# Mixture of experts, one core: the token rows of two expert blocks gathered by one 128-partition indirect DMA instead of two of 64

## The reference, cut to what matters

```python
g_p, g_idx = lax.top_k(g_probs, 1)                 # one of 4 groups
e_p, e_idx = lax.top_k(e_probs, TOP_K)             # two of its 8 experts
expert_idx = g_idx * EXPERTS_PER_GROUP + e_idx     # 32 experts in all
...
# for each expert: its tokens' rows, silu(x @ w_gate) * (x @ w_up) @ w_down,
# weighted and added back to the rows of its tokens
```

## Time and profile before

| | |
|---|---|
| Time, 3 runs | median 2164.02 us (2162.97 to 2166.41) |
| Profiled execution | span 2162.8 us from first to last instruction; its own time isn't listed apart from the span, which lies 0.2 us below the shortest of the 3 runs and 1.2 us below their median |
| PE busy | 2072.4 us, 96% of the span |
| DVE, ACT, POOL busy | 1186.1, 786.0, 176.5 us |
| Granted TensorE clock, mean | 0.986 |
| DMA | 357.61 MB, mean 165 GB/s |
| Expert stage | about 440 to 945 us |

### The profile page before, as it was taken

The page is one execution under the profiler, slowest core; times in us unless marked ns, Lnnn a source line. Parts: engine busy times, 40 slices in busy tenths (PEclk is TensorE's granted clock), DMA queues, the critical chain, the costliest instruction groups (busy, mean ns, idle before and its releaser), DMA issues.

```text
span 2162.8 us, 24857 instructions
## 1 busy us (share of the span) xinstructions
PE 2072.4 (96%) x10090; PEld 1444.9 (67%) x10090; DVE 1186.1 (55%) x1798; ACT 786.0 (36%) x1199; POOL 176.5 (8%) x132
## 2 busy tenths in 40 slices
PE   6999999999999889889999999999999999999997
PEld 4787788843333333348657788888776677888885
DVE  6556534423333233366885864656677858646565
ACT  4546533312211111144673421222345734212233
POOL 1000000010000000000100110102001001101020
PEclk9999999999999999999999999999999999999999
DMA  5342243499999999942202222232222022222221
GB/s 193 117 150 75 78 175 116 157 359 408 406 408 400 398 410 415 421 153 79 72 1 78 90 95 97 87 101 98 96 100 71 2 78 96 95 97 87 101 95 52
DMA packets 41137, 357.61 MB, mean 165 GB/s; under 512 B 6320, under 2 KB 7512, under 8 KB 13376
## 3 DMA queue, kind: packets, MB, share of 16 engines
q1 hardware_dynamic: 36448, 342.99, 41.6%
q0 software_dynamic: 4288, 10.95, 1.7%
q10 hardware_dynamic: 288, 2.10, 0.2%
HBM read 354.94 MB, written 6.83 MB: 167 GB/s over the span
## 4 chain that ended last, share of the span: by engine, by line
PE 81%; DMA 9%; DVE 4%; ACT 3%; issue 2%; SPq 0%; DVEq 0%; ACTq 0%
PE bank L1103 40%; PE bank L2093 10%; PE bank L458 8%; DMA H<-in_expert_up_w 5%; PE bank L473 3%; PE bank L480 2%; DMA AUX<-in_expert_up_w 2%; DMA ring<-in_expert_up_w 2%; PE bank L1885 2%; PE bank L1870 1%; PE bank L1901 1%; PE bank L2118 1%; PE bank L1130 1%; PE bank L2186 1%; ACT S L1950 1%
## 5 line engine op out<-in xcount | busy, mean ns | idle before, releaser
L1103 PE MATMUL bank<-split_x_high,split_weights 128*128 128x512 f32 x1888 | 586.4, 390 | 0.1
L1103 PEld LDWEIGHTS bank<-split_x_high,split_weights 128*128 128x128 f32 x1888 | 354.4, 188 | 76.8 <-issue 3.3
L1364 ACT ACTIVATE split_weights<-ring 128x2048 fp32r<-128x2048 f32 (+1 forms) x113 | 211.1, 1868 | 532.5 <-PE bank L1103 467.7
L1356 DVE TENSOR_TENSOR split_weights<-ring,split_weights 128x2048 fp32r<-128x2048 f32 (+2 forms) x115 | 258.5, 2248 | 164.5 <-ACT split_weights L1364 164.4
L1103 PE MATMUL bank<-split_products,split_weights 128*128 128x512 f32 x1136 | 302.7, 389 | 0.0
L1103 PE MATMUL bank<-split_x_low,split_weights 128*128 128x512 f32 x736 | 286.3, 389 | 0.0
L1103 PEld LDWEIGHTS bank<-split_products,split_weights 128*128 128x128 f32 x1136 | 213.2, 188 | 44.6 <-issue 0.5
L2093 PE MATMUL bank<-split_x_high,split_weights 128*128 128x512 f32 x480 | 153.4, 398 | 6.7 <-DVE split_x_low L2295 6.7
L1103 PEld LDWEIGHTS bank<-split_x_low,split_weights 128*128 128x128 f32 x736 | 138.2, 188 | 28.4
L1080 POOL TENSOR_TENSOR QKVG<-QKVG 128x512 f32<-128x512 f32 x44 | 97.9, 2224 | 551.9 <-DVE QKVG L1567 466.6
L686 DVE SCALAR_TENSOR_TENSOR S<-S,stats,bank 64x512 f32<-64x512 f32 x32 | 23.6, 739 | 197.0 <-ACT S L810 197.0
(11 more groups left out here) (469 smaller groups left out, 3206.6 us busy)
## 6 DMA issues: line engine op xcount, KB each, us to landing
ring<-in_ffn_w_up SPq DMA_DIRECT2D x44, 1024.0 KB, 4.8
ring<-in_w_in SPq DMA_DIRECT2D x24, 1024.0 KB, 4.8
QKVG<-in_expert_gate_w SPq DMA_DIRECT2D x11, 2048.0 KB, 26.4
AUX<-in_expert_up_w SPq DMA_DIRECT2D x11, 2048.0 KB, 31.0
QKVG<-in_expert_down_w SPq DMA_DIRECT2D x11, 2048.0 KB, 33.1
MKV<-in_expert_gate_w SPq DMA_DIRECT2D x11, 2048.0 KB, 30.3
ring<-in_expert_up_w SPq DMA_DIRECT2D x11, 2048.0 KB, 35.8
ring<-in_expert_down_w SPq DMA_DIRECT2D x11, 2048.0 KB, 27.9
```

Of the source, the lines that this page charges most:

```text
L1103: mm = pe.matmul(acc[:, :], w[:, u, k, m], x, start=first and q == 0, stop=last and q == 2)
L1356: st.tell(dve.tensor_tensor(w[:, 1, 0:ks, 0:nc_], raw_half(g)[:, :, 0:nc_], as_f32(w[:, 0, 0:ks, 0:nc_]), ALU.subtract), wl_done)
L1364: st.tell(act.activation(WHL[g % 2][:, 0, 0:ks, 0:nc_], raw_half(g)[:, :, 0:nc_], ACT.Copy), wh_done)
```

## The change

From the fifth block on, one indirect DMA gathers the rows of two blocks: blocks 2i and 2i+1 are pair i, the even one in partitions 0 to 63 and the odd one in 64 to 127. There are two buffers for pairs (`XB_PAIR`): pairs of even number land in `gatew`, those of odd number in `S[:, 8:10, :]`, where all the blocks were before. Blocks 0 to 3 and the further blocks are gathered as before. The index columns of pairs are laid out so that one column of 128 partitions has both lists, which takes two more small writes on DVE. Pair i waits until PE has turned block 2i-3, the last that was read from its buffer. The first pair (i = 2) waits instead until the matmuls of the further lists have read `gatew` (`routed` at 5) and until DVE has passed its own wait for that (`mask_done` at 7). `gathered(b)` says which semaphore and count belong to block b.

```diff
+SINGLE = 4
...
-        idx = sb("idx", [P, EXPERTS], U32)
+        idx = sb("idx", [P, SINGLE // 2 + EXPERTS // 2], U32)
...
-        XB = [S[r, 8:10, :].rearrange("p a n -> p (a n)") for r in XB_ROWS]
+        XB_PAIR = [gatew[:, :, :, :].rearrange("p a b n -> p (a b n)"), S[:, 8:10, :].rearrange("p a n -> p (a n)")]
+        XB = [XB_PAIR[1][r] for r in XB_ROWS]
+
+        def rows_of(b):
+            return XB[b % 2] if b < SINGLE or b >= EXPERTS else XB_PAIR[(b // 2) % 2][XB_ROWS[b % 2]]
+
+        def gathered(b):
+            if b < SINGLE:
+                return xb_landed[b % 2], 16 * (b // 2 + 1)
+            if b < EXPERTS:
+                return xb_landed[(b // 2) % 2], 16 * (b // 4 + SINGLE // 2)
+            return xb_landed[0], 16 * (EXPERTS // 4 + 2 + b - EXPERTS)
...
+            def gather_pair(i, index):
+                pool.indirect_dma_start(XB_PAIR[i % 2], None, rows_dram, bass.IndirectOffsetOnAxis(index, 0), bounds_check=T - 1, oob_is_err=False).then_inc(xb_landed[i % 2], 16)
...
-            for b in range(EXPERTS):
+            for b in range(SINGLE):
                 if b >= 2:
                     pool.wait_ge(x_turned, b - 1)
                 gather(b % 2, idx[0:SLOT, b:b + 1])
+            for i in range(SINGLE // 2, EXPERTS // 2):
+                if i == SINGLE // 2:
+                    pool.wait_ge(routed, 5)
+                    pool.wait_ge(mask_done, 7)
+                else:
+                    pool.wait_ge(x_turned, 2 * i - 2)
+                gather_pair(i, idx[:, SINGLE - SINGLE // 2 + i:SINGLE - SINGLE // 2 + i + 1])
...
-            def turn_x(i):
+            def turn_x(b):
+                r = XB_ROWS[b % 2]
                 for c in range(DC):
-                    mm = pe.transpose(bank[4][:, c * SLOT:(c + 1) * SLOT], XB[i][:, c * P:(c + 1) * P], ident[XB_ROWS[i], XB_ROWS[i]])
+                    mm = pe.transpose(bank[4][:, c * SLOT:(c + 1) * SLOT], rows_of(b)[:, c * P:(c + 1) * P], ident[r, r])
...
-                pe.wait_ge(xb_landed[(b + 1) % 2], 16 * ((b + 1) // 2 + 1))
-                turn_x((b + 1) % 2)
+                pe.wait_ge(*gathered(b + 1))
+                turn_x(b + 1)
...
-            st.tell(dve.tensor_scalar(idx[:, :], bank[7][:, 0:EXPERTS], float(ABSENT), None, ALU.add), mask_done)
+            st.tell(dve.tensor_scalar(idx[:, 0:SINGLE], bank[7][:, 0:SINGLE], float(ABSENT), None, ALU.add), mask_done)
...
                 st.do(dve.tensor_scalar(TOK[r, :], pair_tok, float(ABSENT), None, ALU.add))
+                st.do(dve.tensor_scalar(idx[r, SINGLE:], pair_tok[:, SINGLE // 2:], float(ABSENT), None, ALU.add))
...
                 if b == 2:
                     dve.wait_ge(routed, 5)
+                    st.wait()
+                    dve.sem_inc(mask_done, 1)
```

More of the change, by code:

```diff
@@ L498, in expert_down @@
                 down(b % 2, b % SETS, b % 2 == 0, Y_BANK[b])
-            pe.wait_ge(xb_landed[0], 16)
+            pe.wait_ge(*gathered(0))
             turn_x(0)
@@ L544, in moe_tensor @@
                 down(0, XSET, True)
-                wait_counted(pe, xb_landed[0], j * 16 + 16 * (EXPERTS // 2 + 2))
-                turn_x(0)
+                wait_counted(pe, xb_landed[0], j * 16 + gathered(EXPERTS + 1)[1])
+                turn_x(EXPERTS)
             wait_counted(pe, ys_laid, n_extra * 2 + 2 * EXPERTS)
```

## The result

The changed kernel takes 2147.47 us (median of 4 runs, 2143.68 to 2148.19) against 2165.02 us for the kernel before (4 runs, 2162.97 to 2166.41). The ratio is 0.9917 with a 95% interval of 0.9903 to 0.9931: 17.5 us less, 15 to 21 by the interval. The profiled execution's span went from 2162.8 to 2145.0 us.

A forecast was written before the change was run, and what follows sets the result against it. The prediction took weight transfers to bound the expert blocks, with PE partly idle from 645 us. From 2164.0 us it took off 19.4 lost beside the gathers and added back 2.8, giving 2147.4 us, range 2143 to 2165.

The forecast's parts named there:

- What bounds the stage: Expert blocks: weight transfers bound them; a microsecond of transfer saved between 460 and 925 us comes off the end.
- The loss beside the gathers: 475 to 890 us: weight stream averages 407 GB/s against 427, so 19.4 us lost beside 27 gathers.
- The value taken for the new gathers: Windows of the wide gathers: 2.6% of 108.80 us, so 2.8 us of loss left and 16.6 us gained.
- the choice: Loss nearer to vanishing than staying: an earlier 128-partition transfer ran at 412 GB/s, 64-partition ones at 265.
- PE's idle time: After 645 us: 24.4 us idle before, enough for the 16.6 us gain, shrinking to about 8 us.
- The first pair: Blocks 4 and 5: issued about 475.6 us, landing within 16.4 us, just before block 4's turn at 493.71; cost 0.
- Rows cost what they cost: Rival: loss comes from reading the rows, so 14 gathers lose the 19.4 us again; 2162 to 2165 us, chance 15%.
- half of it stays: Rival: rows may still be moved by other engines than their partition's weights; 9.7 us stays, 2154 us, chance 12%.
- Uneven shares: Rival: 8 of 16 engines move all rows, stage 8.6 us longer and the loss remains; 2172.6 us, chance 13%.

The follow-up runs named there:

- The runs without rows: Lists of blocks 4 to 31 made all absent, gathers still issued: 2138.84 us in the kernel before, 2138.13 us in the changed kernel.
- The run at partitions 32 to 95: Kernel before with all slots of blocks 4 to 31 filled and its 64-partition gathers written, unread, to partitions 32 to 95 of gatew: 2153.63 us.
- the real lists at 32 to 95: Kernel before with its 64-partition gathers written, unread, to partitions 32 to 95 of gatew, lists not filled up: 2152.11 us, ratio 0.9939.
- the run with one block: Changed kernel with 28 gathers, one per block from the fifth, each 128 partitions wide with the other block's 64 slots absent: 2149.02 us.

## Why the prediction was right

**What bounds the stage**: right. Twelve runs in which only the gathers and their lists differ range from 2138 to 2192 us. They fall into groups by the rate of 500 to 850 us: 390 to 396 GB/s goes with 2185 to 2192 us, 407 with 2167, and 424 to 426 with 2138 to 2154, where the number of rows decides as well.

**The loss beside the gathers, 19.4 us**: right in place and near in size. The runs without rows give 25.1 us for rows and loss together, of which 8.1 are bytes: 17.0 us. The rates give 18.5, and the 16 KB packets are longer by 19.0 us per engine in all.

**The value taken for the new gathers**, 2.6% of 108.80 us = 2.8 us: the term was right in kind and too large. The mean rate is 426 against 427, which is 0.9 us over 400. So the gain is 17.5 us where 16.6 were forecast, a difference below what the interval resolves. That the forecast 2147.4 and the measured 2147.47 agree to 0.1 us is luck: the kernel before came out 1.0 us higher in its 4 runs than the 2164.0 that the sum starts from.

**Why the choice was good**: partly by luck. The prediction took 128 against 64 partitions as what tells the two transfers of the earlier trace rows apart. The run at partitions 32 to 95 shows that 64 can be free too. The 128-wide gather with one block's rows, and the real lists at 32 to 95, put nearly all rows of a gather in one half and lose nothing. What they show is that the range of a DMA sets how it is dealt out to the engines. The Trainium skill's rule on ports (SBUF — State Buffer, Door 1: The DMA port swizzle) pointed the right way for this change. But counted by the ports that the present rows reach, these two runs would have kept their loss.

**PE's idle time**: wrong in size. After 645 us it is 264 - 248.52 = 15.5 us, not 8. PE was given more than it seemed: the mean granted clock of the second half rose from 0.96 to 0.99. The lower of the two levels (1.2 and 2.4 GHz) shows in stretches with a wait for weights, as in the window at 678.20 us with 0.79, and three such waits are left of five. The cap on the gain was thus higher than the 24.4 us that I worked out; the run of the changed kernel without rows gained 25.8 (0.9881 on 2164).

**The first pair**: right, with little room. It was issued at 475.40 us; even the longest landing of all gathers, 15.7 us, would give 491.1, and block 4 is turned at 492.28. By the tile view the gather itself took 10.8 us:

```profile
L408 POOL DMA_INDIRECT gatew<-rows_scratch,idx x1: 1023/1023/1023, 475.4 to 475.4; - x1
...
DMA to landing us min/median/max: 10.8/10.8/10.8
```

The prediction's 16.4 us for it was 5.6 too many: it added a whole second window for the odd block's rows, which other engines carry at the same time.

**The rivals**. "Rows cost what they cost" and "half of it stays" are out: 426 GB/s. "Uneven shares" was priced at 8.6 us; the run that has them (real lists at 32 to 95) pays some 5 us, and its blocks with more than 32 rows use the other engines as well. In the changed kernel the even block's rows and the odd block's go to different engines: the 102 rows of its largest pair start within 5.7 us, while 61 rows in one half alone took 5.7 and 7.1 in the run with one block. That was the open question of this rival.

## What to carry to other kernels

Where a stage is bound by weight loads, look at the rate in short windows around each small transfer: a transfer of 128 KB cost three times the time of its bytes here, and no busy share showed it. Before merging or removing small transfers, try the range of partitions that one covers; with all slots filled, 64-partition gathers within one half cost 28 to 30 ns a row and those at 32 to 95 cost 8. And absent rows needn't be avoided: 28 gathers of 128 partitions with one block each took the time of 14 with two, 2149.02 and 2147.47 us, with 1792 absent slots more.

## What the runs showed of the hardware

- An indirect gather of 64 partitions within one half of the partitions lengthens the weight packets of the whole core, also on engines that carry no row of it: from 614 to 688 ns in the median with 7 rows, to 892 and 921 with 61.
- The same rows at partitions 32 to 95, or within a 128-partition range, leave them at 611 to 620 ns in the median of a gather. At 16 to 79, with all slots filled, the time is 2185 us against 2154 at 32 to 95, and the reason is open.
- The shares of an indirect gather, as read from the starts of its rows, are of two neighbouring partitions within a half and of four at 32 to 95 or over 128.
- The record of an absent slot is a 4-byte packet of 9 ns.
- POOL needs 0.94 us to issue 64 indices and 1.00 us for 128.
